# One-hot operands in bf16 with the gates split in two halves, in a two-block transformer kernel on one core

## What is computed

```python
q = (h @ w_q).reshape(B, L, PEER_HEADS, 2, PEER_HALF)        # 8 heads, two halves of 128
s = einsum('blhpd,pnd->blhpn', q, sub_keys)                  # scores against 2 x 128 keys
top_s, top_i = lax.top_k(s, 16)                              # 16 best of either half
cand = top_s[..., 0, :, None] + top_s[..., 1, None, :]       # sums of pairs
best_s, best_pos = lax.top_k(cand, 16)                       # 16 experts of a head
idx = first_index * 128 + second_index                       # of 128 x 128 experts
gate = softmax(best_s)
act = gelu(einsum('bpd,bphkd->bphk', hb, u_tab[ib]))         # first layer, exact gelu
out = einsum('bphk,bphkd->bpd', act * gb, v_tab[ib])         # second layer
```

## Time and profile before

| | |
|---|---|
| median of three runs | 2790.92 us |
| the profiled execution | 2792.14 us |
| its span, first to last instruction | 2790.4 us |
| mean granted TensorE clock | 0.970 |
| busy: TensorE matmul | 2638.9 us (95%) |
| busy: VectorE | 1310.3 us (47%) |
| busy: ScalarE | 909.4 us (33%) |
| busy: GpSimd | 769.8 us (28%) |

### The profile page before, as it was taken

The page is one execution under the profiler, slowest core; times in us unless marked ns, Lnnn a source line. Parts: engine busy times, 40 slices in busy tenths (PEclk is TensorE's granted clock), DMA queues, the critical chain, the costliest instruction groups (busy, mean ns, idle before and its releaser), DMA issues.

```text
span 2790.4 us, 29980 instructions
## 1 busy us (share of the span) xinstructions
PE 2638.9 (95%) x12275; PEld 1598.8 (57%) x12416; DVE 1310.3 (47%) x2249; ACT 909.4 (33%) x1088; POOL 769.8 (28%) x606
## 2 busy tenths in 40 slices
PE   6998988899998889988899999999999999999999
PEld 5776665456776667767344666666444444444444
DVE  6364231412256622249974676767124454443443
ACT  3133422831233331021233545454332322322321
POOL 7674551314241339867664000000000000000000
PEclk9999988998999999999999999999999999999999
DMA  4222221101011112311433444544725555455451
GB/s 165 85 76 76 76 68 57 53 23 62 31 46 46 46 46 95 131 62 58 161 143 137 166 181 167 217 190 181 308 114 211 197 196 223 184 208 214 181 218 53
DMA packets 71432, 359.41 MB, mean 129 GB/s; under 512 B 5488, under 2 KB 38640, under 8 KB 45312
## 3 DMA queue, kind: packets, MB, share of 16 engines
q1 hardware_dynamic: 71296, 357.48, 34.7%
HBM read 286.16 MB, written 71.30 MB: 128 GB/s over the span
## 4 chain that ended last, share of the span: by engine, by line
PE 86%; DVE 7%; ACT 2%; issue 2%; POOL 2%; DMA 0%; SPq 0%; DVEq 0%; ACTq 0%; POOLq 0%
PE ps L696 8%; PE ps L1201 8%; PE ps L1203 8%; PE ps L1202 8%; PE ps L697 8%; PE ps L698 8%; PE ps L1152 8%; PE ps L1151 8%; PE ps L1150 8%; PE ps L1175 4%; PE ps L685 2%; PE ps L1055 2%; PE ps L778 1%; DVE area L2062 1%; PE ps L969 1%
## 5 line engine op out<-in xcount | busy, mean ns | idle before, releaser
L2210 POOL TENSOR_TENSOR wring_parts<-wring,cst 128x512 fp32r<-128x512 f32 (+1 forms) x253 | 291.1, 1181 | 648.2 <-PE ps L698 483.7
L1151 PE MATMUL ps<-sqbuf,wring 128*128 128x512 bf16 x998 | 380.0, 381 | 8.5 <-POOL wring L2235 7.1
L1152 PE MATMUL ps<-sqbuf,wring 128*128 128x512 bf16 x998 | 379.9, 381 | 1.4
L1150 PE MATMUL ps<-sqbuf,wring 128*128 128x512 bf16 x997 | 379.4, 381 | 1.6 <-POOL wring L2235 0.3
L2215 POOL TENSOR_TENSOR wring_parts<-wring,wring_parts 128x512 fp32r<-128x512 f32 (+1 forms) x253 | 341.2, 1378 | 5.3
L2154 DVE TENSOR_TENSOR area<-area 128x4096 bf16<-128x4096 f32 x32 | 141.5, 4425 | 338.6 <-ACT area L1614 338.6
L1614 ACT ACTIVATE area<-area 128x4096 bf16<-128x4096 f32 x32 | 115.6, 3616 | 453.8 <-PE ps L1203 453.8
L696 PE MATMUL ps<-resid_parts,wring_parts 128*128 128x512 f32 (+3 forms) x584 | 229.4, 394 | 8.0 <-DVE normed_x_parts L1715 6.9
L697 PE MATMUL ps<-normed_x_parts,wring_parts 128*128 128x512 f32 (+3 forms) x584 | 226.2, 388 | 0.0
L698 PE MATMUL ps<-resid_parts,wring_parts 128*128 128x512 f32 (+3 forms) x584 | 224.4, 386 | 0.0
L1598 ACT ACTIVATE area<-ps 128x512 f32<-128x512 f32 x128 | 76.3, 597 | 443.1 <-PE ps L1152 443.0
(11 more groups left out here) (236 smaller groups left out, 4571.5 us busy)
## 6 DMA issues: line engine op xcount, KB each, us to landing
wring<-in_weights_dram SPq DMA_DIRECT2D x66, 1024.0 KB, 4.8
area<-in_vT_dram SPq DMA_DIRECT2D x32, 2048.0 KB, 7.8
wring<-in_uT_dram SPq DMA_DIRECT2D x16, 2048.0 KB, 7.7
area<-in_uT_dram SPq DMA_DIRECT2D x16, 2048.0 KB, 9.5
hidden_table<-area SPq DMA_DIRECT2D x32, 1024.0 KB, 4.2
gate_table<-area SPq DMA_DIRECT2D x8, 4096.0 KB, 19.2
normed_x<-gate_table SPq DMA_DIRECT2D x32, 1024.0 KB, 10.4
rt<-hidden_table SPq DMA_DIRECT2D x16, 1024.0 KB, 10.9
```

The source lines that it names most:

```text
L1150: pe.matmul(out, u_hi[:, k, n], h_hi[:, k, :], start=(k == 0), stop=False)
L1151: pe.matmul(out, u_hi[:, k, n], h_lo[:, k, :], start=False, stop=False)
L1152: mm = pe.matmul(out, u_lo[:, k, n], h_hi[:, k, :], start=False, stop=(k == KD - 1))
L2210: ins = nc.gpsimd.tensor_tensor(up[:, d, :], W(name)[:, d, :], C("ones", 0, 1).unsqueeze(1).to_broadcast([P, step, n]), ALU.mult)
```

## The change

The f32 one-hot operands become bf16. The first stays a plain one-hot. The second is held as two products with the gates, one with the gates rounded to bf16 and one with what is left of them (`w_hi`, `w_lo`), side by side, so that one matmul of a token has 128x256 on the moving side, and its two halves of the result are to be added. The result of a quad takes two banks, and there are two such pairs of banks in place of four single ones. ScalarE no longer copies quads: it makes six of a quad's eight gate products (128x128 each, `weigh_gates`), VectorE makes the other two in one instruction, and VectorE adds the halves from PSUM into the stage (`add_quad`, a `tensor_reduce`). One-hots and gate products are made two quads ahead. The quads are spread over 22 groups (8 to 29; five or six each, behind the first three sub-blocks) in place of 16. The lower half of a group's first-layer weights is made in four pieces of 128x1024, one behind each of the first four quads of a group. The loads for the second layer move to group 29, behind the last piece's store, and ScalarE's first work on them to group 30. In `split_group` the upper parts are made by `tensor_copy` with conversion in place of the multiplication by ones.

```diff
@@ -63,9 +63,14 @@
-BEFORE, BESIDE = 8, 16
+BEFORE, BESIDE = 8, 22
 QUADS = T // 4
-QUADS_A_GROUP = QUADS // BESIDE
+def quads_of(g):
+    n = g - BEFORE
+    return range(QUADS * n // BESIDE, QUADS * (n + 1) // BESIDE) if 0 <= n < BESIDE else range(0)
@@ -380,8 +385,11 @@
 ones_at = normed_x[:, :, :].rearrange("p k t -> p (k t)")
-oneA = ones_at[:, 0:16 * P].rearrange("p (a b) -> p a b", a=16)
-oneB = ones_at[:, 16 * P:32 * P].rearrange("p (a b) -> p a b", a=16)
+hot_ring = ones_at[:, 0:32 * P].bitcast(BF16).rearrange("p (z q t n) -> p z q t n", z=4, q=4, t=4)
+oneA, oneB = hot_ring[:, 0], hot_ring[:, 1]
+gateB = ones_at[:, 16 * P:32 * P].bitcast(BF16).rearrange("p (q t z n) -> p q t z n", q=4, t=4, z=2)
+w_lo = rt[:, :, :].rearrange("p a b -> p (a b)")[:, 3 * T:4 * T]
+w_hi = cst[:, CONST["levels"][0]:CONST["levels"][0] + T // 2].bitcast(BF16)
 stage = view(0, 2, 8192)
@@ -540,6 +550,11 @@
+def spread_out(n):
+    at = 4 + 2 * (n % 2)
+    return ps[:, at:at + 2, :].rearrange("p b (t n) -> p (b t) n", t=2)
 block = ctx.enter_context(nc.Block())
@@ -627,9 +642,10 @@
             load_u(g + 4)
-        if BEFORE <= g < BEFORE + BESIDE and (g - BEFORE) % 2:
-            store_piece((g - BEFORE) // 2)
-        if g == BEFORE + BESIDE:
+        for n in quads_of(g):
+            if (n + 1) % (QUADS // PIECES) == 0:
+                store_piece(n // (QUADS // PIECES))
+        if g == BEFORE + BESIDE - 1:
@@ -1167,13 +1183,13 @@
         pe.wait_ge(hot, n + 1)
-        pe.wait_ge(hot_n2, n + 1)
-        if n >= 4:
-            pe.wait_ge(copied, n - 3)
+        pe.wait_ge(hot_gates, n + 1)
+        if n >= 2:
+            pe.wait_ge(copied, n - 1)
         for j in range(4):
-            mm = pe.matmul(ps[:, 4 + q, j * P:(j + 1) * P], oneA[:, 4 * q + j, :], oneB[:, 4 * q + j, :],
-                           start=True, stop=True)
+            mm = pe.matmul(spread_out(n)[:, j, :], oneA[:, q, j, :],
+                           gateB[:, q, j, :, :].rearrange("p z n -> p (z n)"), start=True, stop=True)
         mm.then_inc(spread, 1)
@@ -1214,8 +1230,7 @@
     for g in range(BEFORE, BEFORE + BESIDE):
-        first = QUADS_A_GROUP * (g - BEFORE)
-        pre(g, range(first, first + QUADS_A_GROUP))
+        pre(g, quads_of(g))
     for g in range(BEFORE + BESIDE, GROUPS):
@@ -1597,15 +1612,18 @@
-    def copy_quad(n):
-        piece, i = n // (QUADS // PIECES), n % (QUADS // PIECES)
-        if i == 0 and piece >= 2:
-            act.wait_ge(stored[piece % 2], 16 * (piece // 2))
-        dst = stage[:, piece % 2, :].rearrange("p (j t) -> p t j", t=HALF)
-        act.wait_ge(spread, n + 1)
-        act.activation(dst[:, 4 * i:4 * i + 4, :], ps[:, 4 + n % 4, :].rearrange("p (t j) -> p t j", t=4),
-                       ACT.Copy).then_inc(copied, 1)
+    def weigh_gates(n):
+        q = n % 4
+        act.wait_ge(hot_second, n + 1)
+        if n >= 4:
+            act.wait_ge(spread, n - 3)
+        for i in range(4):
+            t = 4 * n + i
+            ins = act.activation(gateB[:, q, i, 0, :], oneB[:, q, i, :], ACT.Copy, scale=entT[:, 2, t:t + 1])
+            if i < 2:
+                act.activation(gateB[:, q, i, 1, :], oneB[:, q, i, :], ACT.Copy, scale=w_lo[:, t:t + 1])
+        ins.then_inc(hot_gates, 1)
@@ -1631,19 +1649,25 @@
                        ).then_inc(turned_copied, 1)
+    act.wait_ge(turned_copied, TT)
+    act.activation(w_hi, entT[:, 2, :], ACT.Copy).then_inc(gates_rounded, 1)
+    act.wait_ge(gates_split, 1)
+    weigh_gates(0)
+    weigh_gates(1)
     for g in range(BEFORE, BEFORE + BESIDE):
-        first = QUADS_A_GROUP * (g - BEFORE)
         for j in range(EG):
             gelu(g, j)
-            copy_quad(first + 2 * j)
-            copy_quad(first + 2 * j + 1)
-        round_u(g + 2)
+            for n in quads_of(g)[2 * j:2 * j + 2]:
+                if n + 2 < QUADS:
+                    weigh_gates(n + 2)
+        if g + 2 < GROUPS:
+            round_u(g + 2)
     for g in range(BEFORE + BESIDE, GROUPS):
             round_u(g + 2)
-        if g == GROUPS - 3:
+        if g == BEFORE + BESIDE:
@@ -2139,15 +2162,35 @@
             dve.wait_ge(spread, n - 3)
-        dve.tensor_tensor(a, iota, across(0), ALU.is_equal).then_inc(hot_n1, 1)
-        dve.tensor_tensor(b, iota, across(1), ALU.is_equal).then_inc(hot_n2, 1)
-        dve.wait_ge(hot_n1, n + 1)
-        dve.tensor_tensor(a, a, across(2), ALU.mult).then_inc(hot, 1)
-    def split_u(g):
-        dve.wait_ge(u_rounded, g + 1)
-        dve.wait_ge(u_split, g)
-        dve.tensor_tensor(u_hl[g % 2][1], u_raw3[g % 2], u_hl[g % 2][0], ALU.subtract).then_inc(u_split, 1)
+            dve.wait_ge(hot_gates, n - 3)
+        dve.tensor_tensor(oneB[:, q], iota, across(1), ALU.is_equal).then_inc(hot_second, 1)
+        dve.tensor_tensor(oneA[:, q], iota, across(0), ALU.is_equal)
+        dve.wait_ge(hot_second, n + 1)
+        dve.tensor_tensor(gateB[:, q, 2:4, 1, :], oneB[:, q, 2:4, :],
+                          w_lo[:, 4 * n + 2:4 * n + 4].unsqueeze(2).to_broadcast([P, 2, P]), ALU.mult
+                          ).then_inc(hot, 1)
+    def add_quad(n):
+        piece, i = n // (QUADS // PIECES), n % (QUADS // PIECES)
+        if i == 0 and piece >= 2:
+            dve.wait_ge(stored[piece % 2], 16 * (piece // 2))
+        dst = stage[:, piece % 2, :].rearrange("p (j t) -> p t j", t=HALF)
+        out = spread_out(n)
+        dve.wait_ge(spread, n + 1)
+        dve.tensor_reduce(dst[:, 4 * i:4 * i + 4, :], out.rearrange("p t (z n) -> p t n z", z=2), AX_X, ALU.add
+                          ).then_inc(copied, 1)
+    def split_u(g, piece):
+        if piece == 0:
+            dve.wait_ge(u_rounded, g + 1)
+            dve.wait_ge(u_split, g)
+        k = slice(KD * piece // 4, KD * (piece + 1) // 4)
+        ins = dve.tensor_tensor(u_hl[g % 2][1][:, k, :], u_raw3[g % 2][:, k, :], u_hl[g % 2][0][:, k, :],
+                                ALU.subtract)
+        if piece == 3:
+            ins.then_inc(u_split, 1)
@@ -2169,13 +2212,20 @@
     dve.wait_ge(turned_copied, TT)
-    for n in range(QUADS):
+    dve.wait_ge(gates_rounded, 1)
+    dve.tensor_tensor(w_lo, entT[:, 2, :], w_hi, ALU.subtract).then_inc(gates_split, 1)
+    for n in range(2):
         one_hots(n)
-        g = BEFORE + n // QUADS_A_GROUP
-        if n % QUADS_A_GROUP == 1 and g > BEFORE:
-            split_u(g + 1)
+    for g in range(BEFORE, BEFORE + BESIDE):
+        for i, n in enumerate(quads_of(g)):
+            if n + 2 < QUADS:
+                one_hots(n + 2)
+            add_quad(n)
+            if i < 4 and BEFORE < g < GROUPS - 1:
+                split_u(g + 1, i)
     for g in range(BEFORE + BESIDE + 1, GROUPS):
-        split_u(g)
+        for piece in range(4):
+            split_u(g, piece)
     multiply_coefs(0)
@@ -2207,8 +2257,7 @@
         for d in parts:
-            ins = nc.gpsimd.tensor_tensor(up[:, d, :], W(name)[:, d, :],
-                                          C("ones", 0, 1).unsqueeze(1).to_broadcast([P, step, n]), ALU.mult)
+            ins = nc.gpsimd.tensor_copy(up[:, d, :], W(name)[:, d, :])
         ins.then_inc(part_rounded, 1)
```

More of the change, by code:

```diff
@@ L470, in build @@
         stored = [sem(f"stored{i}") for i in range(2)]
-        hot_n1 = sem("hot_n1")
-        hot_n2 = sem("hot_n2")
+        hot_second = sem("hot_second")
+        hot_gates = sem("hot_gates")
+        gates_rounded = sem("gates_rounded")
+        gates_split = sem("gates_split")
         places_hot = sem("places_hot")
@@ L2133, in one_hots @@
                 tokens = slice(4 * n, 4 * n + 4)
-                a, b = oneA[:, 4 * q:4 * q + 4, :], oneB[:, 4 * q:4 * q + 4, :]
                 def across(key):
```

## The result

The changed kernel takes **2742.15 us** (median of four runs, 2739.66 to 2749.51) against 2789.78 us beside it (four runs): a ratio of 0.9836, 95% interval 0.9814 to 0.9858. It is faster by 47.6 us. The forecast was 2748 us, with a range of 2724 to 2785. The profiled execution took 2749.51 us, the highest of the four; its span (from the first to the last instruction) is 42.7 us shorter than that of before, where the steps of the prediction add up to -42.5.

The account below looks back on a forecast made before the run. TensorE, busy 95% of the span, was taken to bound the kernel. The terms -54 + 10 + 1.5 + 9 - 9 = -42.5 us gave 2749.6 from the profiled execution, 2748 us as median, range 2724 to 2785.

Parts of the forecast that it names:

- Quads on TensorE: First-layer groups with quads: a quad takes TensorE 0.47 us instead of 0.89, so 128 quads give -54 us.
- VectorE in a group: Groups of six quads: VectorE keeps up on average, but its order makes TensorE wait 0.5 us in twenty groups, +10 us.
- ScalarE: hidden: Groups with quads: ScalarE's six gate products, 1.8 us a quad, fit beside TensorE's work; 0 us, at worst +5.
- Start of the table: First quads: added rounding and subtraction, partly offset by narrower instructions, make the second quad ready later, +1.5 us.
- SyncE and the tail: Before combine(0): later loads, counted from T (group 29's end on TensorE), make TensorE wait 7 us, then slow matmuls, +9.
- GpSimd's copies: Upper weight parts: 0.6 us a copy instead of 1.02, gaining at first split, contention behind it and first head's selection, -9.
- a rival: VectorE's addition reads PSUM slowly, 2.1 us each, so TensorE waits some 84 us in all: 2822 us, chance 0.15.

Follow-up runs that it names:

- x_beside16: Changed kernel with 16 groups of eight quads again instead of 22 groups of six: 2751.67 us, 0.9866 of the kernel before.
- x_add_twice: Changed kernel with every addition of two gate halves made twice, one behind the other, same output: 2874.15 us, 1.0288 of the kernel before.
- x_one_split: Changed kernel with the lower half of a group's first-layer weights made by one 128x4096 VectorE instruction instead of four pieces: 2813.01 us, 1.0094 of before.
- x_add_first: Changed kernel, but VectorE adds quad n before it makes the one-hots of quad n+2: 2797.78 us, 1.0030 of the kernel before.
- x_all_scalar: Changed kernel with all eight gate products of a quad made on ScalarE, none on VectorE: 2736.97 us, 0.9810 of the kernel before.
- x_splits_first: Changed kernel, but VectorE makes the two second-layer weight splits before multiplying the coefficients, ahead of combine(0): 2737.21 us, 0.9808 of the kernel before.
- the two experiments: GpSimd's converting copy put alone into the kernel before: 2778.43 us; changed kernel with that copy undone to the multiplication by ones: 2757.64 us.
- x_three_ahead: Changed kernel with all gate products on ScalarE, second-layer splits before the coefficient product, and one-hots and products three quads ahead: 2718.80 us, 0.9744 of before.

## Why the prediction was right

**Quads on TensorE: right, a little more.** 0.436 us in place of 0.47; 128 quads by 0.454 are -58, forecast -54. The matmul of 256 columns costs half of one of 512 (0.109), the value that the prediction named and did not take.

**VectorE in a group: right.** Additions of 1.221 us, forecast 1.22. TensorE's waits are 13.0 us in 18, forecast 10 in 20; the longest 0.7, forecast 0.5. x_beside16 and x_add_twice show that VectorE's total sets them, x_one_split and x_add_first that its order does. The rule of the Trainium skill (Advanced Engine Details and Errata, "Memory Cachelines"), that successive values in PSUM should be contiguous, did not show a cost here: the addition reads its pairs 128 values apart at 1221 ns, against 1216 for a reduction of as many values from SBUF.

**ScalarE: hidden, as forecast.** Products of 390 ns; no wait of TensorE is put down to them. x_all_scalar shows how little room was left: with eight a quad they appear at once.

**Start of the table: right.** 8.5 us of waits in place of 6.4, +2.1, forecast +1.5.

**SyncE and the tail: right, each step.** Store landed 14.2 us after its issue, gates issued at T + 15.2 (forecast 15.5), product at T + 35.3 (35), a wait of 7.5 us (7), slow matmuls behind it 1.8 us (2). x_splits_first takes it away (9.5 us) and shows that it is this chain.

**GpSimd's copies: right in the sum, not in its parts.** The profiled executions differ by 9.8 us at the start of the last turning of entries (1501.9 and 1492.1), forecast 9; the medians of the two experiments say 11 and 15. But the selection gave 7.6 us (93.1 to 85.5), not 3. The prediction looked at four instructions of 64 values and counted the other exclusions as hidden. The first split gave 1.7 us (four in 4.75 us against 6.46), not 3 to 4. The first of the gated heads' output projections starts 5.9 us earlier (817.3 against 823.2); from there to the selection 2.5 us are lost again, and behind it 1.2: -5.9 + 2.5 - 7.6 + 1.2 = -9.8.
The Trainium skill (SBUF — State Buffer, "Who interferes with whom") says that a VectorE instruction with two inputs in SBUF contends with a GpSimd instruction that reads SBUF. The trace agrees for the copy: four took 6.80 us with such an instruction of 4.80 us among them, and 2.35 us with short ones.

**Sum.** -58 + 13 + 2.1 + 9.3 - 9.8 = -43.4, and the spans differ by 42.7. Two terms that the sum leaves out nearly cancel: 18 waits by the 0.16 us that their rows leave out are +2.9, and at the start of the table TensorE was busy at a clock of 0.52 for 4.1 us in place of 8.0, some -1.9. The medians differ by 5 us more; that is within their intervals and lies, as far as the experiments tell, in GpSimd's term. That the spans meet the forecast to 1 us is partly luck: two errors in GpSimd's parts cancel, and after's profiled execution was the slowest of its four.

**What was under-priced is a rival.** The addition at 2.1 us was put at 2822 us; by the rate of x_add_twice it would be some 98 us above after, 2840 (an estimate). The term that was missing is the lower clock behind long waits that recur, 30 us in x_add_twice, which the prediction counted for the one wait before combine(0) alone.

## What to carry to other kernels

When work is taken off the engine that bounds and given to one that is nearly full, its total is the smaller question: the order and the length of its single instructions decide, and one instruction of 4.4 us in the wrong place cost more than the whole change gained. Count a stall of TensorE by its length: 39 of up to 1.7 us cost about what they last, 21 of 2.4 us cost two thirds more than they last, because behind 19 of them the matmuls ran at the lower clock. And when a producer's chain is moved later to make room, look at what its consumer needs first: reordering four calls on VectorE, or one group less, gave back by the trace 9.5 and 7.6 us, about what the spread had cost at the end.

## What the runs showed of the hardware that was not expected

A wait's length alone didn't decide whether TensorE's clock fell behind it. In x_one_split 19 of 21 waits of the same 2.4 us had 512-wide matmuls 0.43 us apart behind them, and two had not. In x_add_twice all 18 waits of 3.92 us had them and none of the 21 of 1.68 to 1.75 us. Where they came, they began 0.1 to 1.2 us behind the wait. Why two of the 21 had none stays open. TensorE in time in x_add_twice, behind one wait of 3.92 us, where the slow ones begin with the fourth:

```profile
1726.26 0.60 PE L1192 MATMUL ps<-normed_x 128*128 128x256 bf16 x4 [3.92 <-DVE area L2185]
...
1727.38 0.63 PE L1167 MATMUL ps<-sqbuf,wring 128*128 128x512 bf16 x1
1727.81 0.63 PE L1168 MATMUL ps<-sqbuf,wring 128*128 128x512 bf16 x1
```

The scatter between runs of one kernel has a place. The same instructions ahead of the table, from the first to the last output projection of the gated heads, take 166.7 us in the profile of after and 160.4 in that of x_three_ahead, which doesn't differ there. Over the twelve kernels with GpSimd's copies, none of which differs there, it is 160.4 to 160.6 us in three, 163.7 in two and 166.1 to 166.7 in seven. Part of it is TensorE's clock. A sixth of that stretch, in the one and in the other, with the clock in the third column from the end:

```profile
928.40:956.20 27.80, 25.45 (x120) 19.86 (x119) 14.51 (x23) 6.35 (x14) 0.00 (x0) 0.88 0.11 38
```

```profile
921.70:948.50 26.80, 24.34 (x123) 17.81 (x122) 15.25 (x25) 6.42 (x15) 0.00 (x0) 1.00 0.12 40
```

Why the clock falls there in one execution and not in another stays open; for comparisons of a few microseconds, a mark inside the trace behind it serves better than the total.
